# Hybrid attention and convolution block on one core: ACT takes the second head's exponential behind the first turned chunk's high part

## The chip, the cores and the metric

The kernel runs on one core of one Trainium2 chip. That core has a matmul engine (PE), a vector engine (DVE), an engine for activations (ACT), one for general work (POOL) and a queue that issues the transfers (SP). Each runs its own list of instructions in order, and they wait for each other through semaphores. The metric is the time of one execution in device microseconds. The kernel before took 1782.32 us as the median of 3 runs (1781.41 to 1785.01).

## The reference

One layer on a sequence of 2048 rows of width 1024, in float32:

```python
h = rmsnorm(x, pre_norm_w)
q, k, v, z_att, gb, gc, u, z_conv, g_att, g_conv = split(h @ w_in)
# 4 value heads of width 128; each has two score heads of width 64
sc = einsum(q_block, k) * scale            # rotary q and k; later chunks of 64 keys masked
pr = softmax(sc).reshape(heads, 2, Q_BLOCK, s)
a  = pr[:, 0] - lam * pr[:, 1]             # differential attention
att = rmsnorm(a @ v, subln_w) * 0.8 * silu(z_att)
y_conv = (gb * short_conv(gc * u, conv_w) * silu(z_conv)) @ w_conv_out
m = sigmoid(g_att + b0) * (att @ w_att_out) + sigmoid(g_conv + b1) * y_conv
out = x + rmsnorm(m @ w_out, post_norm_w)
```

Both score heads of a value head are exponentiated, each with its own row maximum and its own row sum. Their rows are then combined into one row of weights, and that row is multiplied with v.

## The kernel before, in words

Matmuls are made from a high and a low part of each float32 operand (hi times hi, hi times lo, lo times hi), so a product is three matmuls, and every operand is split: ACT copies the high part, DVE subtracts it to get the low part.

The program has three stages. First come the projections (until about 735 us). Then comes the attention, with the gate projections as filling between its steps (735 to 1427 us). Last come the two output products (until the end). The change is in the attention stage.

The attention works on 64 tiles G: 4 value heads times 16 blocks of 128 query rows. Tile G has 128 to 2048 keys, in chunks of 512. Every second head goes through its blocks in falling order, so that the number of keys rises and falls smoothly. The work is a pipeline over rounds R, which all engines run through in one written order. In round R:

- PE makes the scores of tile R + 1 (`score`, L1032 and L1033), transposes the combined weights of tile R - 1 chunk by chunk (`turn`, L1043, "turned"), and in even rounds multiplies the turned weights of two tiles with v (`values`, L1060). Between these it puts matmuls of the gate projection (`gates`, L1100), many in odd rounds and few in even ones. The values of chunk c come one step after chunk c was turned, behind the next chunk's turn and scores.
- DVE adds the mask and takes the maximum of each score chunk, writing it to e1 or e2 (`mask_max`, L1629), makes the low part of each turned chunk (`at_split`, at_lo, L1665), combines the two heads of tile R (`combine`, L1643 to L1649; at step 1 of the round), and at the round's end makes the bias for the exponentials of tile R + 1 (`neg_max`, nbias, L1638). In even rounds it also has the low part of a finished output (o_st, L1682), and in odd rounds the normed and gated output (o_n, L1674, and L1678, which reads z_in, a tile that a transfer brings).
- ACT makes the high part of each turned chunk (`at_split`, at_hi, L1322), copies out finished gate units (gate_st, L1351), and takes the exponentials of e1 and e2 over all keys of the tile (`exps`, L1313). In even rounds the output's high part (`o_split`, L1344) comes first, in odd rounds the output's square (`square_o`, L1330).

PE's `turn(R - 1)` waits for `combined`, its `values` for `at_lo_done`; DVE's `at_split` waits for `at_hi_done`, its `combine` for the two exponentials of the tile (`exp_done`). All of it is one chain: scores, maxima, exponentials, combined rows, turned chunks, high part, low part, values. The order within a round on PE is:

```python
for j, (turned_part, scored_part, value_part, part) in enumerate(steps):
    if turned_part:
        turn(R - 1, *turned_part)
    if scored_part:
        for h in range(2):
            score(R + 1, *scored_part, h)
    if value_part:
        values(R - 1, *value_part)
    ...
    gates(part)
```

Line numbers are those of the profile of the kernel before.

Of the kernel before, what the change touches and what calls it, by code (L numbers as in the profile page):

```python
# [8 lines left out]
ACT = mybir.ActivationFunctionType  # L9
# [22 lines left out]
SCALE = HD ** -0.5  # L32
# [38 lines left out]
TILES = VH * NT  # L71
# [179 lines left out]
def units_in(part):  # L251

    return range(part[0] // PER_UNIT, part[1] // PER_UNIT)


def build(nc, t):

    with ExitStack() as whole:
        def sem(name):
            return whole.enter_context(nc.semaphore(name))  # L260

        def held(name, shape, dt=F32, ctx=whole):
            return ctx.enter_context(nc.sbuf_tensor(name, shape, dt))
# [18 lines left out]
        bias = held("bias", [P, GATE_TILES])  # L282
# [73 lines left out]
        nbias = [held(f"nbias{b}", [P, 2], F32, room) for b in range(2)]  # L356
        esum = [held(f"esum{b}", [P, 2], F32, room) for b in range(2)]
# [9 lines left out]
        e2 = [held("e2_0", [P, S], F32, room)]  # L367
        hx = [held(f"hx{i}", [P, 2, BLK], F32R, room) for i in range(SLOTS - KT)]
        e1 = [held("e1_0", [P, S], F32, room)]
# [54 lines left out]
        for k in (2, 3, 4):  # L424
# [42 lines left out]
        mask_ready, exp_done, recip_done, ratio_ready = (  # L467
            sem("mask_ready"), sem("exp_done"), sem("recip_done"), sem("ratio_ready"))
# [704 lines left out]
        def _(act):  # L1173
# [122 lines left out]
            def sigmoids(n, m):  # L1296
                for half in range(2):
                    o = 2 * m + half
                    act.wait_ge(ring_loaded[ring_at(n, o)], 16 * ring_count(n, o))
                    r = ring[ring_at(n, o)][:]  # L1300
                    nc.scalar.activation(r, r, ACT.Sigmoid, bias=bias[:, half * KT + m:half * KT + m + 1]
                                         ).then_inc(gate_ready, 1)
# [3 lines left out]
            nc.scalar.activation(lam[:, 4:6], lam[:, 2:4], ACT.Exp).then_inc(lam_step, 1)  # L1306

            def attend(plan):
                def exps(G):
                    act.wait_ge(nb_ready, G + 1)  # L1310
                    for h, e in enumerate((e1[G % 2], e2[G % 2])):
                        e = e[:, 0:plan.keys(G)]
                        nc.scalar.activation(e, e, ACT.Exp, bias=nbias[G % 2][:, h:h + 1], scale=SCALE,  # L1313
                                             accum_out=esum[G % 2][:, h:h + 1]).then_inc(exp_done, 1)

                def at_split(G, c, wide):
                    if G % 2 == 0 and c == 0 and G:
                        act.wait_ge(pv_done, G // 2)
                    o = plan.before(G) + c // BLK
                    q0 = plan.tile(G)[1] % 2 * P  # L1320
                    act.wait_ge(turned, o + 1)
                    nc.scalar.activation(at_hi[:, c // P:(c + wide) // P, q0:q0 + P],  # L1322
                                         bank[5 + o % 2][:, 0:wide].rearrange("p (k n) -> p k n", n=P), ACT.Copy
                                         ).then_inc(at_hi_done, 1)

                def square_o(B):
                    act.wait_ge(pv_done, B + 1)
                    if B:
                        act.wait_ge(ss_done, B)
                    nc.scalar.activation(o_sq[:], bank[7][:, 0:QB], ACT.Square).then_inc(sq_done, 1)  # L1330

                def inv_root(B):
                    act.wait_ge(ss_done, B + 1)
                    if B:
                        act.wait_ge(o_normed, B)
                    nc.scalar.activation(o_r[:], bank[7][:, QB:2 * QB], ACT.Ln, scale=1.0 / VD).then_inc(ln_done, 1)
                    act.wait_ge(ln_done, B + 1)
                    nc.scalar.activation(o_r[:], o_r[:], ACT.Exp, scale=-0.5).then_inc(r_done, 1)

                def o_split(B):  # L1340
                    act.wait_ge(o_gated, B + 1)
                    if B >= 2:
                        act.wait_ge(att_stored[B % 2], 16 * (B // 2))
                    nc.scalar.activation(o_st[B % 2][:, 0, :].bitcast(F32R), o_n[:], ACT.Copy).then_inc(o_hi_done, 1)  # L1344

                def gates(part):
                    for u in units_in(part):
                        act.wait_ge(unit_done, u + 1)
                        if u >= 2:
                            act.wait_ge(gate_stored[u % 2], 16 * (u // 2))  # L1350
                        nc.scalar.activation(gate_st[u % 2][:], bank[2 + u % 2][:], ACT.Copy).then_inc(gate_out, 1)  # L1351

                gates((0, LEAD))
                for R in plan.rounds:
                    if R % 2 == 0 and 4 <= R <= TILES + 2:
                        o_split((R - 4) // 2)
                    if R % 2 == 1 and 3 <= R <= TILES + 1:
                        square_o((R - 3) // 2)
                    steps = plan.round(R)
                    for j, (turned_part, scored_part, value_part, part) in enumerate(steps):  # L1360
                        if turned_part:
                            at_split(R - 1, *turned_part)
                        if R % 2 == 1 and 3 <= R <= TILES + 1 and j == min(2, len(steps) - 1):
                            inv_root((R - 3) // 2)
                        gates(part)
                    if 0 <= R + 1 < TILES:
                        exps(R + 1)
                for m in range(2):
                    sigmoids(0, m)

            by_plan(act, attend)

            def merge(n):
# [423 lines left out]
```

## Time and profile before

| | |
|---|---|
| median of 3 runs | 1782.32 us (1781.41 to 1785.01) |
| the profiled execution's own time | 1784.02 us |
| its span, first to last instruction | 1782.2 us |
| granted PE clock over the span | 0.996 of full speed |
| PE busy | 1747.7 us, 98% |
| DVE busy | 891.7 us, 50% |
| ACT busy | 581.7 us, 33% |
| POOL busy | 109.3 us, 6% |

How to read it: the busy time is a mean over three stages. What bounds a stage is seen where PE is idle, and in what ended that idle time. The views used are the page, the list of waits, the timeline of single instructions and a table of busy time by stretch. In a timeline row the bracket is the engine's idle time just before the instruction, and behind the arrow stands the instruction or transfer that ended it. The row of an engine that was idle for nothing has no bracket. A row with x2 or more holds several instructions in sequence. The reading of an accumulator, 0.18 to 0.19 us behind each exponential, mostly overlaps it.

### The profile page before, as it was taken

The page shows a single profiled execution, that of the slowest core. Times are in us where ns is not written, and L with a number is a line of the kernel's source. Part 1 is how long each engine was busy: PE and PEld are TensorE (multiplying, and loading weights), DVE is VectorE, ACT ScalarE, POOL GpSimd, SP SyncE. Part 2 cuts the span into 40 slices and gives each one's busy share as a digit, 9 for nine tenths or more (in the row PEclk, how much of TensorE's full clock was granted, in tenths as well). Part 3 has the DMA queues.
Part 4 walks back from the last instruction along what each step waited for, and adds up shares of the span by engine and source line. Part 5 has one row for each costly group of instructions (what it writes and reads, how often), then busy time and mean ns, then how long its engine had stood idle before and what let it go on. Part 6 is the DMA issues. An engine that isn't in the chain of part 4 may idle for free.

```text
span 1782.2 us, 22477 instructions
## 1 busy us (share of the span) xinstructions
PE 1747.7 (98%) x8512; PEld 1460.9 (82%) x8512; DVE 891.7 (50%) x1895; ACT 581.7 (33%) x1040; POOL 109.3 (6%) x82
## 2 busy tenths in 40 slices
PE   7999999999999999999999999999999999999998
PEld 6888888888888888788888887888788878888887
DVE  5527344445334511376666665766666453425242
ACT  5422112121101111245444444444445442313231
POOL 0000000000000000111101112111011030000000
PEclk9999999999999999999999999999999999999999
DMA  6545646465504546976675679657566875353532
GB/s 236 157 177 210 263 165 213 165 213 169 176 23 128 156 120 157 307 226 186 192 214 166 195 236 260 202 172 225 191 210 188 268 267 186 117 179 108 179 107 75
DMA packets 164679, 328.90 MB, mean 185 GB/s; under 512 B 15570, under 2 KB 60626, under 8 KB 159186
## 3 DMA queue, kind: packets, MB, share of 16 engines
q1 hardware_dynamic: 164562, 327.38, 58.3%
q8 instruction: 70, 1.15, 0.3%
q14 instruction: 47, 0.38, 0.1%
HBM read 216.16 MB, written 111.16 MB: 184 GB/s over the span
## 4 chain that ended last, share of the span: by engine, by line
PE 89%; DMA 4%; ACT 3%; DVE 2%; issue 1%; SPq 1%; DVEq 0%; ACTq 0%
PE bank L970 19%; PE bank L971 19%; PE bank L972 19%; PE bank L1100 16%; PE bank L1060 6%; PE bank L1032 3%; PE bank L1033 3%; PE bank L1043 3%; ACT e L1313 2%; DMA q_st<-qk_s 1%; DMA ring<-gate_s 1%; PE bank L1080 1%; DVE at_lo L1665 1%; PE bank L980 1%; PE bank L1077 1%
## 5 line engine op out<-in xcount | busy, mean ns | idle before, releaser
L971 PE MATMUL bank<-ht,w 128*128 128x512 f32 x896 | 348.6, 389 | 0.0
L970 PE MATMUL bank<-ht,w 128*128 128x512 f32 x896 | 348.5, 389 | 0.0
L972 PE MATMUL bank<-ht,w 128*128 128x512 f32 x896 | 348.5, 389 | 0.0
L1100 PE MATMUL bank<-ht,w 128*128 128x512 f32 x912 | 238.2, 395 | 0.5 <-DMA w<-split_s 0.5
L970 PEld LDWEIGHTS bank<-ht,w 128*128 128x128 f32 x896 | 168.2, 188 | 35.0
L972 PEld LDWEIGHTS bank<-ht,w 128*128 128x128 f32 x896 | 168.2, 188 | 34.9
L971 PEld LDWEIGHTS bank<-ht,w 128*128 128x128 f32 x896 | 168.2, 188 | 34.9
L1100 PEld LDWEIGHTS bank<-ht,w 128*128 128x128 f32 x912 | 167.1, 189 | 32.6 <-DMA w<-split_s 0.6
L1629 DVE CUSTOM_DVE_ANT_0 e<-bank,zeros 128x512 f32<-128x512 f32 x192 | 124.8, 688 | 125.3 <-PE bank L1033 125.0
L1313 ACT ACTIVATE e<-e,nbias 128x128 f32<-128x128 f32 (+15 forms) x128 | 152.8, 1197 | 73.1 <-DVE nbias L1638 72.9
L1100 PE MATMUL bank<-hx,w 128*128 128x512 f32 x576 | 154.1, 395 | 0.0
L1322 ACT ACTIVATE at_hi<-bank 128x512 fp32r<-128x512 f32 (+3 forms) x160 | 83.4, 528 | 169.6 <-PE bank L1043 169.4
L1060 PE MATMUL bank<-at_hi,v_sl 128*128 128x256 f32 (+1 forms) x576 | 119.5, 286 | 16.7 <-DVE at_lo L1665 16.5
L1032 PE MATMUL bank<-k_sl,q_st 128*128 128x512 f32 (+3 forms) x320 | 127.4, 403 | 0.4 <-DMA q_st<-qk_s 0.3
L954 POOL TENSOR_SCALAR mask<-kc,qc 128x128 f32<-128x128 f32 (+3 forms) x64 | 87.6, 1369 | 593.2 <-DVE mx L1629 592.7
L1100 PEld LDWEIGHTS bank<-hx,w 128*128 128x128 f32 x576 | 105.0, 189 | 19.5
L1060 PEld LDWEIGHTS bank<-at_hi,v_sl 128*128 128x128 f32 x576 | 96.2, 192 | 28.7 <-DVE at_lo L1665 26.5
L1033 PE MATMUL bank<-k_sl,q_st 128*128 128x512 f32 (+3 forms) x320 | 115.5, 366 | 0.0
L1665 DVE TENSOR_TENSOR at_lo<-bank,at_hi 128x512 fp32r<-128x512 f32 (+3 forms) x160 | 97.1, 607 | 31.6 <-ACT at_hi L1322 31.2
L970 PE MATMUL bank<-br,wa 128*128 128x512 f32 x256 | 99.8, 390 | 1.6 <-DMA wa<-split_s 0.9
L971 PE MATMUL bank<-br,wa 128*128 128x512 f32 x256 | 99.6, 389 | 0.0
L972 PE MATMUL bank<-br,wa 128*128 128x512 f32 x256 | 99.6, 389 | 0.0
(140 smaller groups left out, 2508.5 us busy)
## 6 DMA issues: line engine op xcount, KB each, us to landing
w<-split_s SPq DMA_DIRECT2D x124, 512.0 KB, 4.9
split_s<-piece SPq DMA_DIRECT2D x24, 1024.0 KB, 5.0
q_st<-qk_s SPq DMA_DIRECT2D x128, 128.0 KB, 4.9
gate_s<-gate_st SPq DMA_DIRECT2D x64, 256.0 KB, 5.1
ring<-gate_s SPq DMA_DIRECT2D x64, 256.0 KB, 3.4
raw<-in_w_in SPq DMA_DIRECT2D x28, 512.0 KB, 6.2
ht_s<-ht SPq DMA_DIRECT2D x3, 4096.0 KB, 14.8
qk_s<-stage SPq DMA_DIRECT2D x48, 192.0 KB
```

Of the source, the lines that this page charges most:

```text
L954: nc.gpsimd.tensor_scalar(mask[m % 2][:, 0:wide], kc[:, c:c + wide], qc[:, plan.tile(G)[1]:plan.tile(G)[1] + 1], MASKED, ALU.is_gt, ALU.mu ...
L970: nc.tensor.matmul(out, left[0], right[0], start=start, stop=False)
L971: nc.tensor.matmul(out, left[0], right[1], start=False, stop=False)
L972: return nc.tensor.matmul(out, left[1], right[0], start=False, stop=stop)
L1032: nc.tensor.matmul(out, q_st[G // 2 % 2][:, 0, h, qs], k, start=True, stop=False)
L1033: nc.tensor.matmul(out, q_st[G // 2 % 2][:, 1, h, qs], k, start=False, stop=True).then_inc(qk_done, 1)
L1060: return nc.tensor.matmul(bank[7][:, q0:QB], v, (at_lo if x == 1 else at_hi)[:, k, q0:QB], start=start, stop=stop)
L1100: mm = nc.tensor.matmul(bank[2 + u % 2][:], unit_weights(u)[:, term // 2, k, :], h_slot(bb, k)[:, term % 2, :], start=i == 0, stop=i == PE ...
L1313: nc.scalar.activation(e, e, ACT.Exp, bias=nbias[G % 2][:, h:h + 1], scale=SCALE, accum_out=esum[G % 2][:, h:h + 1]).then_inc(exp_done, 1)
L1322: nc.scalar.activation(at_hi[:, c // P:(c + wide) // P, q0:q0 + P], bank[5 + o % 2][:, 0:wide].rearrange("p (k n) -> p k n", n=P), ACT.Cop ...
L1629: nc.vector.tensor_tensor_reduce(e[:, c:c + wide], bank[(0, 1, 4)[o % 3]][:, 0:wide], mask[m % 2][:, 0:wide] if masked else zeros[:, 0:wid ...
L1665: nc.vector.tensor_tensor(at_lo[:, ks, q0:q0 + P], bank[5 + o % 2][:, 0:wide].rearrange("p (k n) -> p k n", n=P), at_hi[:, ks, q0:q0 + P]. ...
```

## The change

In the kernel before, `exps(G)` takes both heads of a tile one after the other at the end of round G - 1. In the changed kernel `exps(G, h)` takes one head. Head 0 stays at the end of round G - 1. Head 1 is taken in round G, in the first step, behind the high part of the first turned chunk (or at that place in the list where nothing is turned).

```diff
--- before.py
+++ after.py
@@ -1306,12 +1306,11 @@
             nc.scalar.activation(lam[:, 4:6], lam[:, 2:4], ACT.Exp).then_inc(lam_step, 1)
 
             def attend(plan):
-                def exps(G):
+                def exps(G, h):
                     act.wait_ge(nb_ready, G + 1)
-                    for h, e in enumerate((e1[G % 2], e2[G % 2])):
-                        e = e[:, 0:plan.keys(G)]
-                        nc.scalar.activation(e, e, ACT.Exp, bias=nbias[G % 2][:, h:h + 1], scale=SCALE,
-                                             accum_out=esum[G % 2][:, h:h + 1]).then_inc(exp_done, 1)
+                    e = (e2 if h else e1)[G % 2][:, 0:plan.keys(G)]
+                    nc.scalar.activation(e, e, ACT.Exp, bias=nbias[G % 2][:, h:h + 1], scale=SCALE,
+                                         accum_out=esum[G % 2][:, h:h + 1]).then_inc(exp_done, 1)
 
                 def at_split(G, c, wide):
                     if G % 2 == 0 and c == 0 and G:
@@ -1360,11 +1359,15 @@
                     for j, (turned_part, scored_part, value_part, part) in enumerate(steps):
                         if turned_part:
                             at_split(R - 1, *turned_part)
+                        if j == 0 and 0 <= R < TILES:
+
+
+                            exps(R, 1)
                         if R % 2 == 1 and 3 <= R <= TILES + 1 and j == min(2, len(steps) - 1):
                             inv_root((R - 3) // 2)
                         gates(part)
                     if 0 <= R + 1 < TILES:
-                        exps(R + 1)
+                        exps(R + 1, 0)
                 for m in range(2):
                     sigmoids(0, m)
```

The instructions and their number are the same, and the order on the four other engines is the same. What moves on ACT is the second exponential of each of the 64 tiles. The next rows are ACT's list at the start of round 16 (an even round). In the names, e1_0 and e2_0 are the score rows of the two heads of tile 16, the digit is the buffer, o_st0 is the output's high part, and bank5 and bank6 hold turned chunks in turn. Before:

```order
L1313 ACTIVATE e1_0,esum0<-e1_0,nbias0 128x2048 [waits nb_ready]
L1313 ACTIVATE e2_0,esum0<-e2_0,nbias0 128x2048
L1344 ACTIVATE o_st0<-o_n 128x256 [waits att_stored0,o_gated]
L1322 ACTIVATE at_hi<-bank5 128x4x128 [waits turned]
L1322 ACTIVATE at_hi<-bank6 128x4x128 [waits turned]
```

In the changed kernel:

```order
L1312 ACTIVATE e1_0,esum0<-e1_0,nbias0 128x2048 [waits nb_ready]
L1343 ACTIVATE o_st0<-o_n 128x256 [waits att_stored0,o_gated]
L1321 ACTIVATE at_hi<-bank5 128x4x128 [waits turned]
L1312 ACTIVATE e2_0,esum0<-e2_0,nbias0 128x2048 [waits nb_ready]
L1321 ACTIVATE at_hi<-bank6 128x4x128 [waits turned]
```

The exponential of e2_0 has moved down past o_st0 and past the first high part, and stands in front of the second high part.

The next rows are the same list at the start of round 17 (an odd round), where o_sq is the output's square and gate_st1 a finished gate unit. Before:

```order
L1313 ACTIVATE e1_1,esum1<-e1_1,nbias1 128x1920 [waits nb_ready]
L1313 ACTIVATE e2_1,esum1<-e2_1,nbias1 128x1920
L1330 ACTIVATE o_sq<-bank7 128x256 [waits ss_done,pv_done]
L1322 ACTIVATE at_hi<-bank5 128x4x128 [waits turned,pv_done]
L1322 ACTIVATE at_hi<-bank6 128x4x128 [waits turned]
```

In the changed kernel:

```order
L1312 ACTIVATE e1_1,esum1<-e1_1,nbias1 128x1920 [waits nb_ready]
L1329 ACTIVATE o_sq<-bank7 128x256 [waits ss_done,pv_done]
L1321 ACTIVATE at_hi<-bank5 128x4x128 [waits turned,pv_done]
L1312 ACTIVATE e2_1,esum1<-e2_1,nbias1 128x1920 [waits nb_ready]
L1321 ACTIVATE at_hi<-bank6 128x4x128 [waits turned]
```

Here the exponential of e2_1 has moved down past o_sq and past the first high part, whose instruction waits for `turned`.

## Rows read from the trace of the kernel before

**Rows 1.** Page, parts 1 and 5: busy us (share) xinstructions; group xcount | busy, mean ns | idle before.
```profile
PE 1747.7 (98%) x8512; PEld 1460.9 (82%) x8512; DVE 891.7 (50%) x1895; ACT 581.7 (33%) x1040; POOL 109.3 (6%) x82
...
L1313 ACT ACTIVATE e<-e,nbias 128x128 f32<-128x128 f32 (+15 forms) x128 | 152.8, 1197 | 73.1 <-DVE nbias L1638 72.9
```

**Rows 2.** Waits of PE and of ACT, attention stage: total us, times, longest us.
```profile
PE bank L1060 <- DVE at_lo L1665: 16.5, 17, 2.8
...
ACT at_hi L1322 <- PE bank L1043: 169.4, 91, 4.4
```

**Rows 3.** Timeline of round 16: start us, us, engine line op out<-in xcount [idle before <-releaser].
```profile
904.97 2.01 ACT L1313 ACTIVATE e<-e,nbias 128x2048 f32<-128x2048 f32 x1 [0.93 <-DVE nbias L1638]
905.74 0.60 PE L1043 MATMUL bank<-ident,e 128*128 128x128 f32 x4
906.97 2.00 ACT L1313 ACTIVATE e<-e,nbias 128x2048 f32<-128x2048 f32 x1
908.95 0.40 ACT L1344 ACTIVATE o_st<-o_n 128x256 fp32r<-128x256 f32 x1
909.26 1.06 ACT L1322 ACTIVATE at_hi<-bank 128x512 fp32r<-128x512 f32 x2
909.87 0.69 DVE L1665 TENSOR_TENSOR at_lo<-bank,at_hi 128x512 fp32r<-128x512 f32 x1 [1.58 <-ACT at_hi L1322]
910.62 0.50 PE L1060 MATMUL bank<-at_hi,v_sl 128*128 128x256 f32 x2 [1.05 <-DVE at_lo L1665]
912.03 0.69 DVE L1665 TENSOR_TENSOR at_lo<-bank,at_hi 128x512 fp32r<-128x512 f32 x1
914.21 0.28 PE L1060 MATMUL bank<-at_hi,v_sl 128*128 128x256 f32 x1
```

**Rows 4.** Timeline of PE: its other waits before the first value matmuls, same columns.
```profile
749.39 0.45 PE L1060 MATMUL bank<-at_hi,v_sl 128*128 128x256 f32 x2 [0.87 <-DVE at_lo L1665]
...
877.22 0.51 PE L1060 MATMUL bank<-at_hi,v_sl 128*128 128x256 f32 x2 [0.95 <-DVE at_lo L1665]
...
943.83 0.50 PE L1060 MATMUL bank<-at_hi,v_sl 128*128 128x256 f32 x2 [1.85 <-DVE at_lo L1665]
...
972.81 0.50 PE L1060 MATMUL bank<-at_hi,v_sl 128*128 128x256 f32 x2 [0.23 <-DVE at_lo L1665]
...
978.70 0.38 PE L1060 MATMUL bank<-at_hi,v_sl 128*128 128x256 f32 x1 [0.36 <-DVE at_lo L1665]
...
1038.49 0.50 PE L1060 MATMUL bank<-at_hi,v_sl 128*128 128x256 f32 x2 [0.26 <-DVE at_lo L1665]
...
1053.64 0.51 PE L1060 MATMUL bank<-at_hi,v_sl 128*128 128x256 f32 x2 [0.97 <-DVE at_lo L1665]
...
1076.94 0.69 PE L1060 MATMUL bank<-at_hi,v_sl 128*128 128x256 f32 x2 [2.82 <-DVE at_lo L1665]
...
1285.09 0.79 PE L1060 MATMUL bank<-at_hi,v_sl 128*128 128x256 f32 x2 [2.71 <-DVE at_lo L1665]
...
1396.34 0.50 PE L1060 MATMUL bank<-at_hi,v_sl 128*128 128x256 f32 x2 [1.20 <-DVE at_lo L1665]
```

**Rows 5.** Timeline of ACT and DVE: what stood in front of five of these.
```profile
747.91 0.60 ACT L1313 ACTIVATE e<-e,nbias 128x384 f32<-128x384 f32 x1
...
940.39 1.78 ACT L1313 ACTIVATE e<-e,nbias 128x1792 f32<-128x1792 f32 x1
...
1052.89 0.69 DVE L1665 TENSOR_TENSOR at_lo<-bank,at_hi 128x512 fp32r<-128x512 f32 x1 [0.18 <-ACT at_hi L1322]
...
1075.52 0.42 DVE L1678 TENSOR_TENSOR o_n<-o_n,z_in 128x256 f32<-128x256 f32 x1 [4.80 <-DMA z_in<-z_s]
...
1395.59 0.69 DVE L1665 TENSOR_TENSOR at_lo<-bank,at_hi 128x512 fp32r<-128x512 f32 x1 [0.41 <-ACT at_hi L1322]
```

**Rows 6.** Busy time by stretch: from:to, us, PE, PEld, DVE, ACT, POOL, PEclk, DMA share, GB/s.
```profile
1076.00:1084.00 8.00, 6.72 (x24) 5.58 (x24) 3.60 (x17) 2.20 (x8) 2.34 (x1) 0.57 1.06 294
1284.00:1288.00 4.00, 2.91 (x12) 2.82 (x13) 3.59 (x10) 0.80 (x2) 0.00 (x0) 0.57 0.02 6
```

## The prediction

> **What bounds the kernel now.** I read the page first. PE is busy for 98% of the span and ACT for a third [rows 1], so a change on ACT can only pay where ACT makes PE wait. The list of PE's waits, cut to the attention stage, has one entry of size: 16.5 us in 17 waits of the value matmuls (L1060) for a low part (L1665), the longest 2.8 us [rows 2]. Then I went through the timeline to see what stood in front of each of the 17.
>
> Round 16 shows the usual case [rows 3]. ACT starts the pair of exponentials at 904.97. PE turns the first chunk of the previous tile at 905.74, so its high part could be made from about 906.3. But ACT is in the pair until 908.95, then makes o_st, and only at 909.26 the high part. DVE has been idle for 1.58 us when it can start the low part at 909.87, and PE has been idle for 1.05 us when the values start at 910.62. The second exponential, 2.00 us long, lay in the middle of this chain, although nobody needed its result before DVE's `combine` of the next step.
>
> The other waits are in [rows 4]. They lie in even rounds, where PE has few gate matmuls to fill with. The rounds 33 to 63 repeat the key counts of 1 to 31, and most of their waits too: 0.95, 1.05 and 0.26 us (rounds 14, 16, 26) come twice with the same length, 0.23 and 0.36 (both in round 20) come again as 0.27 and 0.36. Round 18 has 1.85 and its twin 2.71, round 28 has 0.97 and its twin 1.20. Alone stand round 2 (0.87), round 32 (2.82) and round 56 (0.36). Together that is 16.5.
>
> **The change part by part.** Nothing is added or removed: 64 second exponentials of 1197 ns in the mean [rows 1] change their place on ACT, 76.6 us of ACT time in all. No other engine's list changes, so SP's queue is not reordered.
>
> What it brings. In the rounds with a wait the first high part comes earlier by one exponential, but PE gets no more than the least of three numbers: the length of that exponential, DVE's idle time before the low part (if DVE was busy, ACT was not the cause), and PE's own wait. Where the last of these decides, the wait is gone:
> - rounds 14, 16 and twins: the exponentials are 1.9 to 2.0 us, so 0.95 and 1.05 go in full, twice: 4.0 us.
> - rounds 18 and 50: the exponential is 1.78 us [rows 5], shorter than both waits, 1.85 and 2.71. Gain 1.78 each: 3.56 us. 0.07 and 0.93 stay.
> - round 20 and twin: 0.23 and 0.27 go: 0.5 us. The 0.36 later in the same round has DVE working through without idle time since the first low part. DVE starts earlier, and so does PE. Between nothing and 0.36 each; I take 0.2, the nearer to the middle: 0.4 us.
> - round 2: an exponential of 0.60 us [rows 5]: 0.6 us. Round 56: 0.36.
> - rounds 28 and 60: DVE was idle for only 0.18 and 0.41 us before these low parts [rows 5]; the rest of the wait is its two maxima. Gain 0.6 us of 2.17.
> - round 26 and twin (0.26 each): DVE's low part followed the maxima with no idle time. Nothing.
> - round 32 (2.82): DVE stood 4.80 us in front of the transfer of z_in [rows 5]. No exponential is in the way. Nothing.
>
> Sum: 4.0 + 3.56 + 0.5 + 0.4 + 0.6 + 0.36 + 0.6 = 10.0 us.
>
> The clock adds to this. In the 4 us around the wait of 2.71 the granted clock is 0.57 in the mean, that is a stretch at 1.2 instead of 2.4 GHz, and PE is busy for 2.91 us of it [rows 6]: about 2.91 x 0.43 = 1.3 us lost. The other 15 waits, the one of 1.85 us among them, cost no clock that I could see: over the whole span it is 0.996, and these two stretches account for nearly all that is missing (8 x 0.43 + 4 x 0.43 = 5.2 us of 7). With 0.93 us of waiting left the clock should stay up in round 50: 1.3 us. Sum 11.3 us. The other fall, at round 32, costs 6.72 x 0.43 = 2.9 us [rows 6] and stays with its wait.
>
> What it costs. In every round the second exponential now ends later: behind o_st or o_sq and one high part, some 1 us, and behind PE's turn where that is late. Queued behind it stand the second chunk's high part and the gate copy. In round 16 I get this: first exponential until 907.0, o_st until 907.4, high part until 908.0, second exponential until 910.1, second high part until 910.7. DVE took up the second low part at 912.03 and PE needed it at 914.21 [rows 3]; with everything about a microsecond earlier that is 911 and 913. So the second high part hides behind DVE's maxima, with 0.3 us to spare for DVE and over 1.5 us for PE. If that cover were gone, PE would lose up to the 2.0 us of one exponential in a wide even round. In the odd rounds gate matmuls stand between the steps, and no value matmuls follow. I cost all this at nothing; the bounds are 0 and the 0.3 us of spare in each of the 16 even rounds with three or more turned chunks, 4.8 us. I take 0, since in the row DVE began the second low part 1.3 us after the time at which the high part would now be ready.
>
> The profiled execution took 1784.0 us, which gives 1772.7. It was 1.7 us above the median of the runs shown, so I predict 1771.0.
>
> **A rule weighed.** In the odd rounds ACT often waits for the turn: 169.4 us in 91 waits, up to 4.4 us [rows 2], and now a long instruction that would be ready stands behind that wait. The Trainium skill (TensorE: Matmul & The Clock Gate, "Architectural detail: the array is 16x 32x32, not 1x 128x128") says that ACT's and DVE's queues are strictly first in, first out. The trace agrees as far as it shows it: ACT's idle time before the high part is charged to the turn although later instructions of its list were ready. By that rule alone the change is a loss of cover, and this is the fourth rival.
>
> **The rivals.**
> 1. The gain before round 32 is given back to the transfers. Some 5 us of the 10 fall before it (0.6 + 0.95 + 1.05 + 1.78 + 0.23 + 0.2 + 0.18). Around round 32 the transfer engines are fully busy, share 1.06 [rows 6]. If z_in lands at the same absolute time as now, PE waits 5 us longer there. Against it: SP issues these transfers when PE and DVE have come so far, so they should move along. Time 1771.0 + 5.0 = 1776.
> 2. The wait at round 32 goes too, because the transfers fall a little otherwise: 2.8 us of waiting and 2.9 us of clock, 1771.0 - 5.7 = 1765.3. For it: the wait is an accident of one burst, as its twin stages have none. Against it: nothing in the change aims at it.
> 3. The change doesn't do what it says for PE: the low part is held by DVE's list rather than by ACT, as in rounds 26 and 28, and only a microsecond or two comes: 1781. Against it stand DVE's idle microseconds before the low part in the wide rounds.
> 4. Slower. The second exponential, held behind the turn, ends too late for DVE's `combine`, which stands in front of the next maxima; these hold back PE's scores, and the combined row comes late for the next turn. It decides from the point where the second exponential ends later than DVE has finished the second low part. The price is the high part of about 0.6 us by which it is pushed: in half of the 62 rounds 31 x 0.6 = 18 us: 1771.0 + 18 = 1789. Against it: in round 16 the exponential would end at 910.1, two microseconds before that low part.
>
> **How the numbers follow.** The forecast 0.66, rival 1 0.12, rival 2 0.10, rival 3 0.05, rival 4 0.07. The forecast's own range is 1769 to 1776 (its unknown terms: 0.3 us down, 4.8 up, and a microsecond or so of the measurement). With rivals 1 and 2 taken in, the range is 1765 to 1779. A measurement of this kernel tells about 0.2% or 3.6 us from no change, so faster means below 1778.7: forecast, rival 2 and nearly all of rival 1, 0.87. Within 0.2%: rival 3 and a weak form of the forecast, 0.08. Slower 0.05, since a part of rival 4 would only eat the gain.
>
> **What would show it.** PE's waits for the low part should fall from 16.5 us to about 6, with round 32's 2.8 the longest and nothing left in rounds 14, 16, 46 and 48. The granted clock should stay full in round 50. DVE's idle time for the high part should shrink in the wide even rounds. ACT's idle time for the bias (72.9 us [rows 1]) and for the turn may move, at no price. I am wrong if PE shows new waits in its transposes (L1043) or scores, or waits for the low part of a second chunk, or a longer one at round 32.

## The result, and the profile after

The changed kernel took 1770.27 us as the median of 6 runs (1767.66 to 1771.18), the kernel before 1783.66 us (1781.41 to 1786.08, 6 runs). The ratio is 0.9923 with an interval of 0.9912 to 0.9934, and the medians are 13.4 us apart. The forecast was 1771.0, with a gain of 11.3 us. So the time was met more closely (0.7 us) than the gain (2.1 us). That is luck: the forecast started from a median of three runs (1782.32), and the six runs put the kernel before 1.3 us higher.

The profiled execution of the changed kernel was the fastest of its six (1767.66 us), that of before took 1784.02. Some of the 16.4 us between these two is thus luck of the execution, and the comparison below says which part. DVE's lines are 3 higher in the changed kernel (the low part is L1668), ACT's are 1 lower (the exponential is L1312, the high part L1321).

The page of the changed kernel, with the two rows that answer to [rows 1]:

```profile
PE 1741.4 (99%) x8512; PEld 1459.0 (83%) x8512; DVE 890.1 (50%) x1895; ACT 585.0 (33%) x1040; POOL 109.4 (6%) x82
...
L1312 ACT ACTIVATE e<-e,nbias 128x128 f32<-128x128 f32 (+15 forms) x128 | 153.7, 1201 | 69.8 <-DVE nbias L1641 69.6
```

The exponentials are as many and as long as before. The first and the third stage take the same time in both to within 0.2 us; the difference is in the attention stage. A table of busy time by stretch (stretch; its length; busy us and instructions of PE, PEld, DVE, ACT, POOL; granted clock; share of the transfer engines; GB/s) has that stage in one row, before:

```profile
735.00:1426.31 691.31, 673.68 (x3734) 572.88 (x3732) 447.92 (x1280) 313.76 (x606) 85.75 (x62) 0.99 0.69 212
```

and after:

```profile
735.00:1409.98 674.98, 666.93 (x3735) 570.48 (x3733) 446.47 (x1280) 316.90 (x606) 85.71 (x62) 1.00 0.70 217
```

691.31 - 674.98 = 16.3 us. PE's idle time in it falls from 17.6 to 8.1 us, but PE's busy time falls as well, by 6.8 us for the same work. Both halves are explained below.

The list of waits of the changed kernel (engine, line, what it waited for: total us, times, longest us), against [rows 2]:

```profile
ACT at_hi L1321 <- PE bank L1043: 159.8, 101, 4.4
...
DVE at_lo L1668 <- ACT at_hi L1321: 13.2, 13, 3.0
...
PEld bank L1060 <- DVE at_lo L1668: 10.5, 19, 1.8
...
PE bank L1060 <- DVE at_lo L1668: 5.1, 9, 1.3
...
DVE o_n L1681 <- DMA z_in<-z_s: 4.6, 3, 3.3
...
PE bank L1032 <- DMA q_st<-qk_s: 2.7, 2, 1.7
```

PE's 16.5 us for the low part have become 5.1. The same list of the kernel before has two more rows to set beside it:

```profile
DVE at_lo L1665 <- ACT at_hi L1322: 31.2, 31, 3.0
...
PEld bank L1060 <- DVE at_lo L1665: 26.5, 28, 3.2
```

So DVE waits for ACT's high part in 13 places instead of 31. PEld, the loading of PE's weights, waited in 28 places before where PE showed only 17. That is one of the two places where the forecast was short, as will be seen.

The timeline of round 16 in the changed kernel, from the first exponential to the second chunk's values, answers to [rows 3]:

```profile
902.76 2.01 ACT L1312 ACTIVATE e<-e,nbias 128x2048 f32<-128x2048 f32 x1 [0.93 <-DVE nbias L1641]
...
903.54 0.60 PE L1043 MATMUL bank<-ident,e 128*128 128x128 f32 x4
...
904.76 0.40 ACT L1343 ACTIVATE o_st<-o_n 128x256 fp32r<-128x256 f32 x1
...
905.07 0.57 ACT L1321 ACTIVATE at_hi<-bank 128x512 fp32r<-128x512 f32 x1
...
905.55 1.99 ACT L1312 ACTIVATE e<-e,nbias 128x2048 f32<-128x2048 f32 x1
...
906.01 0.69 DVE L1668 TENSOR_TENSOR at_lo<-bank,at_hi 128x512 fp32r<-128x512 f32 x1
...
906.97 0.40 PE L1033 MATMUL bank<-k_sl,q_st 128*128 128x512 f32 x1
...
907.20 0.39 PE L1060 MATMUL bank<-at_hi,v_sl 128*128 128x256 f32 x2
...
907.54 0.58 ACT L1321 ACTIVATE at_hi<-bank 128x512 fp32r<-128x512 f32 x1
...
908.30 0.69 DVE L1668 TENSOR_TENSOR at_lo<-bank,at_hi 128x512 fp32r<-128x512 f32 x1
...
908.90 0.15 DVE L1646 RECIPROCAL ratio<-esum 128x1 f32<-128x1 f32 x1
...
910.68 0.28 PE L1060 MATMUL bank<-at_hi,v_sl 128*128 128x256 f32 x1
```

Counted from the start of the first exponential, the first high part stands at 2.31 us; before it stood at 4.29. DVE goes from its maxima to the low part without an idle bracket, and PE goes from the scores to the values without one. The second exponential ends at 907.54. The second low part, at 908.30, has no bracket either, and `combine` (L1646), which needs that exponential, starts 1.4 us after its end. PE meets the second chunk's values 2.4 us after their low part began.

What is left of PE's long idle times, from the timeline of PE, answers to [rows 4]:

```profile
751.92 0.50 PE L1032 MATMUL bank<-k_sl,q_st 128*128 128x512 f32 x1 [0.98 <-DMA q_st<-qk_s]
...
1032.16 0.50 PE L1060 MATMUL bank<-at_hi,v_sl 128*128 128x256 f32 x2 [0.26 <-DVE at_lo L1668]
...
1047.05 0.50 PE L1060 MATMUL bank<-at_hi,v_sl 128*128 128x256 f32 x2 [0.71 <-DVE at_lo L1668]
...
1068.86 0.45 PE L1060 MATMUL bank<-at_hi,v_sl 128*128 128x256 f32 x2 [1.34 <-DVE at_lo L1668]
...
1073.01 0.44 PE L1032 MATMUL bank<-k_sl,q_st 128*128 128x384 f32 x1 [1.71 <-DMA q_st<-qk_s]
...
1271.47 0.50 PE L1060 MATMUL bank<-at_hi,v_sl 128*128 128x256 f32 x2 [1.20 <-DVE at_lo L1668]
```

In this order these are round 3 (a new wait, for a transfer), round 26 (0.26, unchanged), round 28 (0.97 before), round 32 with its two (2.82 and 0.33 before) and round 50 (2.71 before). Rounds 14, 16, 18, 46 and 48 have none. Not shown are the waits of rounds 58 and 60 (0.26 and 0.71, as in their twins 26 and 28), 0.23 in each of rounds 20 and 52, and 0.16 in round 50. The stretches at rounds 32 and 50, the table answering to [rows 6]:

```profile
1068.00:1076.00 8.00, 5.43 (x29) 4.61 (x30) 4.52 (x22) 3.30 (x12) 3.06 (x2) 1.00 1.08 313
1271.00:1275.00 4.00, 3.53 (x23) 3.17 (x24) 3.92 (x10) 2.55 (x4) 0.00 (x0) 1.00 0.19 67
```

The clock is full in both, where it was 0.57.

**Where the 16.4 us came from.** I compared the start of each round's `neg_max` in the two traces. The table gives by how much the changed kernel's lead grew in the rounds named (worked out from 64 pairs of starts), beside the forecast's term.

| rounds | lead gained, us | forecast, us |
|---|---|---|
| 14, 16, 46, 48 | 1.24, 1.32, 1.24, 1.32 = 5.1 | 4.0 |
| 18 | 1.7 | 1.8 |
| 50 and 51, clock and wait together | 2.4 | 1.8 + 1.3 |
| 20, 21 and 52, 53 | 1.3 | 0.9 |
| 12, 22, 24, 44, 54 | 0.27, 0.21, 0.27, 0.27, 0.22 = 1.2 | 0 |
| 28 and 60 | 0.7 | 0.6 |
| 2 and 3 | 0.93 - 0.73 = 0.2 | 0.6 |
| 56 | 0.5 | 0.36 |
| 32 to 34 | 2.7 | 0 |
| start of the stage and its last round | 0.6 | 0 |
| sum | 16.4 | 11.3 |

The odd rounds that are not named gained nothing.

### The profile page after: what moved, and what is told of

Same layout as the page of the kernel before. It is cut to its first block, busy times and chain, and to the rows that moved or that the text cites. A ratio compares the mean times of both kernels' runs of the same rounds, so it can differ in the third digit from the quotient of the medians.

```text
span 1765.8 us, 22477 instructions
## 1 busy us (share of the span) xinstructions
PE 1741.4 (99%) x8512; PEld 1459.0 (83%) x8512; DVE 890.1 (50%) x1895; ACT 585.0 (33%) x1040; POOL 109.4 (6%) x82
## 4 chain that ended last, share of the span: by engine, by line
PE 92%; DMA 4%; DVE 1%; SPq 1%; issue 1%; ACT 1%; DVEq 0%; ACTq 0%
PE bank L970 19%; PE bank L972 19%; PE bank L971 19%; PE bank L1100 17%; PE bank L1060 5%; PE bank L1032 3%; PE bank L1033 3%; PE bank L1043 3%; DMA q_st<-qk_s 1%; DMA z_in<-z_s 1%; DMA ring<-gate_s 1%; PE bank L980 1%; PE bank L1080 1%; PE bank L1077 1%; DMA qk_s<-stage 1%
## 5 line engine op out<-in xcount | busy, mean ns | idle before, releaser
L1312 ACT ACTIVATE e<-e,nbias 128x128 f32<-128x128 f32 (+15 forms) x128 | 153.7, 1201 | 69.8 <-DVE nbias L1641 69.6
L1321 ACT ACTIVATE at_hi<-bank 128x512 fp32r<-128x512 f32 (+3 forms) x160 | 84.9, 531 | 160.2 <-PE bank L1043 159.8
L1668 DVE TENSOR_TENSOR at_lo<-bank,at_hi 128x512 fp32r<-128x512 f32 (+3 forms) x160 | 97.0, 606 | 13.2 <-ACT at_hi L1321 13.2
```

The lines of the kernel that those rows point to most:

```text
L1668: nc.vector.tensor_tensor(at_lo[:, ks, q0:q0 + P], bank[5 + o % 2][:, 0:wide].rearrange("p (k n) -> p k n", n=P), at_hi[:, ks, q0:q0 + P]. ...
```

## The experiments

The kernel before ran beside them with a median of 1785.02 us (29 runs, with the first four) and 1785.63 us (17 runs, with the last four). Each experiment is given with its ratio to it. The changed kernel's ratio is 0.9923. The diffs are against the changed kernel, but for one that says otherwise.

### 1. Only the even rounds

```diff
-                        if j == 0 and 0 <= R < TILES:
+                        if j == 0 and 0 <= R < TILES and R % 2 == 0:
                             exps(R, 1)
...
                     if 0 <= R + 1 < TILES:
                         exps(R + 1, 0)
+                        if (R + 1) % 2 == 1:
+                            exps(R + 1, 1)
```

> Second exponential moved behind the first high part in the 32 even rounds only; in the odd rounds the pair stays together in front. My theory (the gain comes from even rounds, where the values follow one step behind the turn): the same as the changed kernel, ratio to before 0.9925, within 0.001. Rival (odd rounds carry part of the gain, through the output's square coming earlier or DVE starting earlier): 0.994 to 0.996. Rival (the move costs something in odd rounds, through the exponential held behind PE's turn): faster than the changed kernel, 0.990 to 0.9915.

Measured: 1770.83 us (1768.56 to 1772.67), ratio 0.9912 (0.9898 to 0.9927). PE's waits in it:

```profile
PE bank L1060 <- DVE at_lo L1668: 6.3, 11, 2.4
...
PE bank L1032 <- DMA q_st<-qk_s: 3.7, 2, 2.6
```

The even rounds carry the whole gain. The ratio itself lies in the range that I had given to a cost in the odd rounds, but its interval holds the changed kernel's 0.9923 too, and the rounds decide it. Round by round this execution runs in step with the profiled one of the changed kernel, except in four places: it loses 1.6 us at the start, 0.6 in rounds 2 and 3 and 3.5 in rounds 32 to 34, where it waits for transfers, and is 0.3 us better in round 50. None of them is touched by the odd rounds' order.

### 2. Only the odd rounds

```diff
-                        if j == 0 and 0 <= R < TILES:
+                        if j == 0 and 0 <= R < TILES and R % 2 == 1:
                             exps(R, 1)
...
+                        if (R + 1) % 2 == 0:
+                            exps(R + 1, 1)
```

> The move in the 32 odd rounds only. My theory: no change against before, ratio 0.999 to 1.001, since filling matmuls stand between the steps there. Rival one: 0.996 to 0.998. Rival two (a cost there): 1.001 to 1.003.

Measured: 1785.08 us (1783.46 to 1787.18), ratio 0.9999 (0.9989 to 1.0008). In the odd rounds the later place neither brings nor costs anything that can be measured.

```profile
PE bank L1060 <- DVE at_lo L1668: 14.7, 17, 2.5
```

This run also had something that I had not asked for. The waits of rounds 18 and 50 are as before, here from the timeline of PE:

```profile
944.29 0.50 PE L1060 MATMUL bank<-at_hi,v_sl 128*128 128x256 f32 x2 [1.85 <-DVE at_lo L1668]
...
1284.52 0.50 PE L1060 MATMUL bank<-at_hi,v_sl 128*128 128x256 f32 x2 [2.55 <-DVE at_lo L1668]
```

But the clock fell behind the shorter one, in round 18, and stayed full behind the longer one, in round 50 (the table by stretch, the clock is the third number from the end):

```profile
944.00:948.00 4.00, 3.71 (x16) 3.32 (x17) 3.93 (x10) 0.00 (x0) 0.00 (x0) 0.61 0.01 2
...
1284.00:1288.00 4.00, 3.48 (x23) 3.13 (x24) 3.93 (x10) 0.83 (x2) 0.00 (x0) 1.00 0.01 5
```

In the kernel before it was the other way round.

### 3. Behind the output's high part only

The second exponential stands behind o_st or o_sq, but still ahead of the first turned chunk's high part.

```diff
                     for j, (turned_part, scored_part, value_part, part) in enumerate(steps):
+                        if j == 0 and 0 <= R < TILES:
+                            exps(R, 1)
                         if turned_part:
                             at_split(R - 1, *turned_part)
-                        if j == 0 and 0 <= R < TILES:
-
-
-                            exps(R, 1)
```

> The second exponential goes behind the output's high part or square, but stays in front of the first turned chunk's high part. My theory: the high part comes no earlier than before, so nothing is gained, ratio 0.999 to 1.001, and PE's waits for the low part stay near 16 us in 17. Rival (it is the earlier output work that helps, or the split of the pair as such): 0.994 to 0.997.

Measured: 1783.68 us (1781.21 to 1786.97), ratio 0.9991 (0.9982 to 1.0).

```profile
PE bank L1060 <- DVE at_lo L1666: 14.8, 17, 2.9
...
PE bank L1032 <- DMA q_st<-qk_s: 2.9, 2, 2.5
```

The 17 waits are all there. Their sum is 1.7 us smaller, and that lies in rounds 2 (0.28 us instead of 0.87) and 32 (1.54 instead of 2.82), which differ from execution to execution. If there is a gain it is under a fifth of a per cent. What pays is the step past the high part.

### 4. Six rounds undone

```diff
-                        if j == 0 and 0 <= R < TILES:
+                        if j == 0 and 0 <= R < TILES and R not in (14, 16, 18, 46, 48, 50):
                             exps(R, 1)
...
+                        if R + 1 in (14, 16, 18, 46, 48, 50):
+                            exps(R + 1, 1)
```

> The changed kernel with the move undone in rounds 14, 16, 18, 46, 48 and 50 only. In the two traces the changed kernel's lead grew there by 1.24, 1.32, 1.73, 1.24, 1.32 and 2.4 to 2.7 us, together 9.3 to 9.6. My theory: these come back, ratio to before 0.9975 to 0.9985, 9 to 10 us slower than the changed kernel, with a low granted clock in round 50 again. Rival (the lead is made elsewhere, and the leads of single rounds are an accident of the two executions): within 4 us of the changed kernel, 0.9925 to 0.995.

Measured: 1782.2 us (1777.88 to 1784.3), ratio 0.9979 (0.9969 to 0.9989). That is 0.0056 or 10 us above the changed kernel, and 0.0067 or 12 us above experiment 1, which was measured in the same set: the six rounds hold most of the gain. Round by round, the changed kernel's lead over this one grows by 1.23, 1.32, 1.74, 1.22, 1.32 and 1.36 us, 8.2 together. The forecast's terms without the clock were 4.0 + 3.56 = 7.6. Of the 2 to 4 us between 8.2 and the ratios, about one is the clock, which falls in some executions (below). The remainder is about as large as the two ratios are uncertain (0.0010 and 0.0011 to 0.0015, together some 3 us).

The clock did not do what I expected. Round 50 has its wait again, and the clock stays full:

```profile
PE bank L1060 <- DVE at_lo L1668: 12.0, 14, 2.6
```

```profile
1283.00:1287.00 4.00, 3.50 (x23) 3.14 (x24) 3.93 (x10) 0.81 (x2) 0.00 (x0) 1.00 0.01 2
```

In the third experiment the same stretch reads so:

```profile
1283.00:1287.00 4.00, 3.47 (x14) 3.07 (x15) 3.93 (x10) 0.24 (x1) 0.00 (x0) 0.59 0.01 4
```

PE is busy for as long, but with 14 instructions in place of 23. This is how a lower clock looks in a count.

### 5. z_in a round earlier, in the kernel before

Theory: at round 32 DVE stands 4.8 us in front of z_in, so an earlier z_in takes PE's 2.8 us away. The diff is against the kernel before, on SP:

```diff
-                    if R % 2 == 0 and 2 <= R <= TILES:
-                        B = R // 2 - 1
+                    if R % 2 == 1 and 1 <= R <= TILES - 1:
+                        B = (R - 1) // 2
```

> The kernel before, with the transfer of z_in issued one round earlier. My theory: DVE's wait of 4.80 us for it at round 32 goes, and with it PE's 2.82 us and the 2.9 us of clock behind it; PE's small wait for q_st there may grow by 1 to 2 us. 3 to 6 us faster than before, ratio 0.9965 to 0.998. Rival (the burst of transfers holds PE in any case, by the next thing it lacks): no change, 0.999 to 1.001.

Measured: 1786.13 us (1783.36 to 1789.74), ratio 1.0005 (0.9996 to 1.0015). My theory fell. The wait for z_in is gone, but at the same place PE now waits for its own transfer, in the timeline of PE:

```profile
1081.23 0.69 PE L1032 MATMUL bank<-k_sl,q_st 128*128 128x384 f32 x1 [3.69 <-DMA q_st<-qk_s]
```

```profile
1076.00:1088.00 12.00, 8.31 (x28) 6.82 (x27) 4.23 (x17) 2.33 (x9) 1.95 (x2) 0.72 1.10 280
```

The transfer engines are full there, share 1.10. My reading is that what is issued earlier pushes back what is issued behind it; one pair of traces doesn't prove that, since PE's wait for q_st at this place differs between executions in any case, from 0.33 to 2.88 us in the eight profiles with the old order of transfers. What the profiles do show is the sum of PE's two waits there, for the low part and for q_st: 3.05 to 4.98 us in those eight, 3.69 in this run and 2.94 in the next, where the first of the two waits is gone.

### 6. z_in a round earlier, in the changed kernel

The same edit on the changed kernel.

> The changed kernel with the same earlier transfer. In its trace DVE waits 3.33 us and PE 1.34 us there, at full clock, and then 1.71 us for q_st. My theory: 1 to 2 us faster than the changed kernel, ratio to before 0.9915 to 0.992. Rival: no change against it, since the wait for q_st takes the place.

Measured: 1772.38 us (1768.69 to 1777.09), ratio 0.9926 (0.991 to 0.9943). No gain over the changed kernel, against my theory again. All of PE's wait at round 32 is for q_st now (2.9 us):

```profile
PE bank L1032 <- DMA q_st<-qk_s: 4.7, 2, 2.9
...
PE bank L1060 <- DVE at_lo L1668: 4.2, 9, 1.4
```

### 7. The second exponential one step later still

It stands behind the second turned chunk's high part, where there is one.

```diff
-                        if j == 0 and 0 <= R < TILES:
+                        if j == min(1, len(steps) - 1) and 0 <= R < TILES:
                             exps(R, 1)
```

> The second exponential goes one step later still, behind the second turned chunk's high part (in rounds of one step it stays). It puts the rival of the prediction to the test: the exponential ends too late for the combining of the heads. By hand for round 16: the second high part ends at 906.8, the exponential at 908.8, the combining starts at 908.9 now, so no loss in the wide even rounds; in the odd rounds it ends some 2 us after PE's second turn, where DVE takes the low part 1.8 us after it, so DVE waits up to a microsecond and PE hardly. My theory: 0 to 2 us slower than the changed kernel, ratio to before 0.9925 to 0.994. Rival (there is no slack behind the second exponential): 5 us or more slower than the changed kernel, 0.995 or more.

Measured: 1770.85 us (1769.01 to 1771.96), ratio 0.9912 (0.9899 to 0.9926), not to be told from the changed kernel, where I had expected up to 2 us more. Its timeline of round 16, ACT and DVE (two lines higher here):

```profile
909.12 0.60 ACT L1321 ACTIVATE at_hi<-bank 128x512 fp32r<-128x512 f32 x1 [0.82 <-PE bank L1043]
...
909.62 2.00 ACT L1312 ACTIVATE e<-e,nbias 128x2048 f32<-128x2048 f32 x1
...
910.95 0.69 DVE L1666 TENSOR_TENSOR at_lo<-bank,at_hi 128x512 fp32r<-128x512 f32 x1
...
911.73 0.16 DVE L1644 RECIPROCAL ratio<-esum 128x1 f32<-128x1 f32 x1
```

The exponential now ends at 911.62, just as DVE is done with the second low part, and `combine` starts 0.11 us later. Here the cover is used up, and still PE loses nothing. In three other places it is overdrawn: the list of DVE's waits has `combine` waiting for the exponential 3 times, 0.9 us in all and 0.4 us at the longest. In the changed kernel 1.4 us of it are left.

### 8. The low part between the two maxima

In rounds 26 and 28 DVE's maxima stood in front of the low part. This takes the low part between them, in the first step of the even rounds.

```diff
+                        early = R % 2 == 0 and j == 0
                         if scored_part:
-                            for h in range(2):
-                                mask_max(R + 1, *scored_part, h)
-                        if turned_part:
+                            mask_max(R + 1, *scored_part, 0)
+                        if early and turned_part:
+                            at_split(R - 1, *turned_part)
+                        if scored_part:
+                            mask_max(R + 1, *scored_part, 1)
+                        if turned_part and not early:
                             at_split(R - 1, *turned_part)
```

> The changed kernel, and DVE makes the first low part of an even round between the two maxima of that step instead of behind both. What is left of PE's waits for the low part (5.1 us in 9) is in rounds where DVE was busy with the maxima: 0.71 twice, 0.26 twice. My theory: these go, 1.5 to 3 us faster than the changed kernel, ratio to before 0.991 to 0.992. Rival (the later second maximum holds back a score's bank or the low part waits for ACT with the maximum behind it): no gain or 1 to 3 us slower, 0.9925 to 0.994.

Measured: 1770.49 us (1768.56 to 1772.91), ratio 0.9909 (0.9895 to 0.9923), not to be told from the changed kernel, and not from my theory's 0.991 to 0.992 either. Round 26's wait is gone and round 28's is down from 0.71 to 0.27 us; against the changed kernel this execution gains 1.3 us in rounds 25 to 31 and 0.8 in rounds 57 to 61. But the second maximum stands behind the low part now, and PE waits in round 18 for a later low part where it had not, which costs 0.5 us:

```profile
946.74 0.39 PE L1060 MATMUL bank<-at_hi,v_sl 128*128 128x256 f32 x1 [0.66 <-DVE at_lo L1668]
```

At round 32 it is 3.3 us behind, with waits for transfers. So the rounds show a gain of one to two microseconds, and the times are too rough to confirm it.

## Why the prediction was right, and where its sizes were off

**The mechanism.** The forecast was that a second exponential, which nobody needed yet, stood in front of the first high part, and that PE's values waited behind it. The changed kernel's round 16 shows each link gone. Experiment 3 moves the exponential past everything but the high part and keeps the 17 waits; experiment 4 puts it back in six rounds and gives back 10 us. The sums of the forecast hold, but for a rounding in rival 4 (31 x 0.6 is 18.6). Experiments 1 and 2 place the whole effect in the even rounds, as forecast.

**Rounds 14, 16, 46 and 48 (4.0 forecast, 5.1 found)** are the mis-sized term. Read in the trace, PE waited 0.95 and 1.05 us. The round got shorter by 1.24 and 1.32. The 0.27 to 0.29 us more are in the rows. Before, PE's last score matmul ahead of the wait reads:

```profile
909.17 0.40 PE L1033 MATMUL bank<-k_sl,q_st 128*128 128x512 f32 x1
```

and the values start at 910.62. In the changed kernel the same matmul starts at 906.97, and the values start at 907.20. In flow the next one starts 0.23 us behind it, so 0.17 of its 0.40 us is the end of the pipeline, which a following matmul would have overlapped; in front of a wait it counts as busy. After the wait the first pair of values takes 0.50 us and in flow 0.39: another 0.1. Both are costs of the wait that stand as busy time. They are also a part of the 6.8 us by which PE's busy time fell: the clock makes 4.2 of these (1.3 and 2.9 by the forecast's reckoning of the two stretches), and some 2.5 are left for such ends and starts.

**Rounds 12, 22, 24, 44 and 54 (nothing forecast, 1.2 found)** are the same thing. I looked only where PE had an idle bracket. In round 12 of the kernel before, only the loading of weights has one:

```profile
846.87 0.30 PEld L1060 LDWEIGHTS bank<-at_hi,v_sl 128*128 128x128 f32 x2 [0.43 <-DVE at_lo L1665]
846.88 0.50 PE L1060 MATMUL bank<-at_hi,v_sl 128*128 128x256 f32 x2
```

The matmul's 0.50 gives the stop away, and the round got 0.27 us shorter. In rounds 22, 24, 44 and 54 the weight loads waited 0.27, 0.45, 0.43 and 0.28 us; in the changed kernel four of the five waits are gone and 0.17 is left in round 24. The two effects together are 1.1 + 1.2 = 2.3 us. The waits without the clock came to 12.1 us (the table's 16.4, less 2.7 for round 32, 0.6 for the start and 1.0 for the clock) where I had 10.0; the small terms of rounds 2, 50, 20, 28 and 56 were off by 0.1 to 0.4 each, in both directions.

**Rounds 18 and 50.** I took the exponential's 1.78 us for each. Round 18 gained 1.7, and its last 0.07 us of waiting went too. Round 50 gained 1.36 against experiment 4, where the clock was full on both sides. Its wait fell to 1.20, not to 0.93. The missing 0.3 us are not the exponential's. In round 50 ACT comes late to the first exponential, because the copy of a gate unit in front of it waits until the store of an earlier unit has landed. Before and after:

```profile
1279.38 0.60 ACT L1351 ACTIVATE gate_st<-bank 128x512 f32<-128x512 f32 x1 [2.83 <-DMA gate_s<-gate_st]
...
1267.53 0.60 ACT L1350 ACTIVATE gate_st<-bank 128x512 f32<-128x512 f32 x1 [3.08 <-DMA gate_s<-gate_st]
```

PE's wait follows this one in all ten profiles. In the five with the old order in this round, ACT waits 2.66, 2.73, 2.83, 2.97 and 3.00 us and PE 2.55, 2.62, 2.71, 2.86 and 2.89, always 0.11 or 0.12 less. In the five with the new order ACT waits 2.69, 2.76, 2.87, 3.08 and 3.24 and PE 0.82, 0.89, 1.00, 1.20 and 1.37, always 1.87 or 1.88 less. The difference of the two, 1.76 us, is the exponential's length (1.78) to within 0.02: the forecast's term was right, and the store took 0.25 us more in this pair of executions. It is also why round 50 waited longer than its twin, round 18, and why a wait of about 1 us is left in it. The forecast had not seen that.

**The clock (1.3 forecast).** The loss was real in the profiled execution of before, and its end was worth about 1.0 us (2.4 for rounds 50 and 51, less 1.36). In experiment 2, with the fall behind the same 1.85 us in round 18, rounds 18 and 19 took 1.3 us longer than before. But I had tied it to the length of one wait, and that was wrong. Five of the profiled executions have the waits of both rounds: in two the clock fell in round 50, behind waits of 2.71 (before) and 2.86 (experiment 3); in one in round 18, behind 1.85 (experiment 2); in two in neither, behind 1.85 and 2.62 (experiment 4) and 2.07 and 2.89 (experiment 5). In the five executions with the changed order in these rounds it never fell there. So the change does take this loss away, but the loss comes in some executions and not in others: 1.0 to 1.3 us in three of five is about 0.7 us on average. What decides in the single execution the runs do not tell.

**Round 32 (nothing forecast).** The profiled execution gained 2.7 us there: DVE's wait for z_in is 3.3 us instead of 4.8, PE's is 1.34 instead of 2.82, its wait for q_st 1.71 instead of 0.33, and the clock stays full. I don't count this to the change. The execution of experiment 1 is 3.5 us slower in the same rounds with the same order in the even ones, and the clock is low there in six of the ten profiles, to different depths. It is a burst of transfers that falls differently each time. Against the medians the account closes without it: 12.1 + 0.7 = 12.8 us, where 13.4 was measured, and the ratio's interval is 2 us to either side.

**The rivals.** Rival 1, the gain given back at round 32, did not come: the lead was 6.6 us in front of that round and 9.3 behind it. The transfers move along with the work, as SP issues them by how far PE and DVE have come: the z_in that DVE waits for there was issued at 1057.90 instead of 1064.34. In rounds 2 and 3 it may have come in small: 0.93 us were gained and 0.73 lost in a wait for q_st. But PE has such a wait of 0.39 to 0.81 us in experiments 2, 3 and 5 too, where round 2 has the old order, so two single executions don't show it. Rival 2 came by half in this execution, by chance and not by the change. Rival 3 is refuted by the gain itself and by experiment 4. Rival 4, the exponential too late for `combine`, is refuted by experiment 7, which spends the cover and is no slower. The rule of strict order that I had weighed (the Trainium skill, TensorE: Matmul & The Clock Gate, "Architectural detail: the array is 16x 32x32, not 1x 128x128") holds in these traces: in round 17 of the changed kernel ACT stands idle for 1.01 us in front of the high part, waiting for the turn, and the second exponential, whose bias was ready since the round before, starts only behind it. It costs nothing that can be measured, since experiment 2 has it in all odd rounds at a ratio of 0.9999. What I had left at nothing stayed at nothing.

**What stays open.** Why the clock falls behind one wait and not behind an equal one; and how PE's wait of 3 to 5 us at round 32 could be taken away. Experiments 5 and 6 only moved it to another transfer. Fewer bytes at that place, or a longer lead for all of them, were not tried. Nor was anything against round 50's wait of about 1 us behind the store of a gate unit.

## What to carry to other kernels

When an engine is idle two thirds of the time and another waits for it, look at what its list holds in front of the instruction waited for. If that is long and its own reader is far away, put it behind: a reordering of one engine gave 0.77% here. Price such a wait by more than the bracket on the matmul: about 0.27 us more for each stop on this kernel, and look at the weight loads for stops too short to leave a bracket.

## What the runs showed of the hardware

In rounds 18 and 50 the granted clock fell from 2.4 GHz to its lower level, 1.2 GHz (0.57 to 0.61 in the mean over 4 us, as a part of them ran at full clock), at the end of or just behind waits of PE of 1.85, 2.71 and 2.86 us, and did not fall at waits of 1.85, 2.07, 2.55, 2.62 and 2.89 us in the same rounds. At round 32 the six falls came with waits of 2.58 to 3.69 us, and the four profiles without a fall had waits of 2.53 us at most. A fall cost 1.0 to 1.3 us. Waits near 1 us cost no clock in the attention stage of any of the ten profiles. A transfer issued a round earlier while the transfer engines were full (share 1.06 to 1.10) saved nothing: PE's wait for the low part went (2.82 us before), and its wait for q_st was 3.69 us in one run and 2.94 in the other. A wait of PE costs more than its idle bracket: where PE's bracket was 0.95 or 1.05 us, the round got 1.24 or 1.32 us shorter without it.
